# Mamba-2 layer of a diffusion trunk: z's in-projection tiles between the scan's steps, cumulated sums loaded by DMA, one exponential for both directions

## What is computed

```
proj = h @ w_in                       # z: 2048 columns, x: 2048, B: 1024, C: 1024, dt: 64
xbc  = silu(depthwise_conv(proj[x, B, C]))
dt   = softplus(dt_raw + dt_bias);  a = -exp(a_log)
# ssd_scan, for each direction, over chunks of 128 tokens, 8 groups of 4 heads:
acs    = cumsum(dt * a)                             # inside the chunk
decay  = exp(where(i >= j, acs_i - acs_j, -inf))
y_diag = ((C_i . B_j) * decay * dt_j) @ x
state  = state * exp(acs_last) + (exp(acs_last - acs) * dt * x)^T @ B
y_off  = (C_i . state) * exp(acs_i)
y      = rms_norm((y_f + flip(y_b) + x * skip) * silu(z), norm_g) @ w_out
```

## Time and profile before

| | us |
|---|---|
| median of 3 runs (2195.01 to 2195.77) | 2195.66 |
| the profiled execution: its own time | 2194.43 |
| its span, first to last instruction | 2192.7 |
| mean granted clock of PE over it | 0.959 |

### The profile page before, as it was taken

How to read it: one execution, slowest core, us unless ns; L and a number is a source line. 1 busy time by engine, 2 the same in 40 slices (tenths; PEclk the granted TensorE clock), 3 DMA queues, 4 the chain that set the end, 5 groups by cost and what they waited for, 6 DMA issues and landing times.

```text
span 2192.7 us, 30627 instructions
## 1 busy us (share of the span) xinstructions
PE 1998.8 (91%) x11880; PEld 1795.2 (82%) x11880; DVE 1295.2 (59%) x1942; ACT 976.0 (45%) x1703; POOL 745.2 (34%) x567
## 2 busy tenths in 40 slices
PE   3789999999978877999999995799999979899998
PEld 1579998799978866799987994599998766699986
DVE  0567761666338866677724797377751686577732
ACT  1344442544336633544424683354442535544432
POOL 0133324333326655333343730233334330333242
PEclk7889999999989989999999997999999988999999
DMA  9953346434310034544365500644446432244332
GB/s 371 383 208 124 124 132 233 165 124 125 125 58 30 31 121 173 221 144 125 116 230 175 203 11 0 278 173 125 125 164 221 147 111 82 81 145 125 125 125 77
DMA packets 77072, 320.96 MB, mean 146 GB/s; under 512 B 8672, under 2 KB 14208, under 8 KB 63104
## 3 DMA queue, kind: packets, MB, share of 16 engines
q1 hardware_dynamic: 76048, 318.18, 41.4%
q10 hardware_dynamic: 880, 0.82, 0.1%
HBM read 314.96 MB, written 4.01 MB: 145 GB/s over the span
## 4 chain that ended last, share of the span: by engine, by line
PE 72%; DVE 14%; ACT 5%; DMA 5%; issue 2%; POOL 1%; SPq 1%; DVEq 0%; ACTq 0%
PE pair L1675 15%; PE pair L1677 15%; PE pair L1676 15%; PE pair L1709 6%; PE pair L1711 6%; PE pair L1710 6%; DVE convolved L1484 5%; PE pair L1798 2%; DVE x L1246 2%; DMA mod_more<-in_w_mod 1%; PE pair L1831 1%; DMA raw<-in_pool 1%; DMA raw<-in_ssd_out 1%; ACT junk L848 1%; DVE w_lo L1179 1%
## 5 line engine op out<-in xcount | busy, mean ns | idle before, releaser
L675 POOL TENSOR_TENSOR w_lo<-raw,w_hi 128x512 fp32r<-128x512 f32 (+1 forms) x375 | 578.0, 1543 | 1205.9 <-ACT w_hi L820 1205.9
L1675 PE MATMUL pair<-h_hi,w_hi 128*128 128x386 f32 (+1 forms) x2008 | 686.6, 342 | 19.4 <-POOL h_lo L682 19.4
L1677 PE MATMUL pair<-h_hi,w_lo 128*128 128x386 f32 (+1 forms) x2008 | 682.6, 340 | 0.0
L1676 PE MATMUL pair<-h_lo,w_hi 128*128 128x386 f32 (+1 forms) x2008 | 681.9, 340 | 0.0
L1179 DVE TENSOR_TENSOR w_lo<-raw,w_hi 128x512 fp32r<-128x512 f32 x351 | 427.7, 1221 | 335.7 <-ACT w_hi L820 335.7
L820 ACT ACTIVATE w_hi<-raw 128x1024 fp32r<-128x1024 f32 x375 | 393.0, 1050 | 293.6 <-PE pair L1711 208.7
L1675 PEld LDWEIGHTS pair<-h_hi,w_hi 128*128 128x128 f32 (+1 forms) x2008 | 380.1, 189 | 24.2 <-POOL h_lo L682 22.9
L1676 PEld LDWEIGHTS pair<-h_lo,w_hi 128*128 128x128 f32 (+1 forms) x2008 | 380.7, 190 | 0.9
L1677 PEld LDWEIGHTS pair<-h_hi,w_lo 128*128 128x128 f32 (+1 forms) x2008 | 380.1, 189 | 0.3
L1303 DVE SCALAR_TENSOR_TENSOR acc<-pair,taps,acc 128x385 f32<-128x385 f32 x176 | 108.9, 619 | 212.6 <-ACT acc L907 212.6
L907 ACT ACTIVATE acc<-pair,taps 128x386 f32<-128x386 f32 x176 | 117.4, 667 | 236.1 <-PE pair L1677 236.1
(11 more groups left out here) (254 smaller groups left out, 2481.6 us busy)
## 6 DMA issues: line engine op xcount, KB each, us to landing
raw<-in_ffn_in SPq DMA_DIRECT2D x176, 512.0 KB, 3.5
raw<-in_ffn_out SPq DMA_DIRECT2D x88, 512.0 KB, 3.6
mod_raw<-in_w_mod SPq DMA_DIRECT2D x32, 1024.0 KB, 7.6
mod_base<-in_w_mod SPq DMA_DIRECT2D x31, 1024.0 KB, 7.5
mod_more<-in_w_mod SPq DMA_DIRECT2D x20, 1024.0 KB, 13.4
raw<-in_ssd_conv SPq DMA_DIRECT2D x32, 512.0 KB, 3.5
gb<-rows_dram SPq DMA_DIRECT2D x8, 1024.0 KB, 5.2
raw<-in_ssd_z SPq DMA_DIRECT2D x16, 512.0 KB, 3.5
```

Source lines behind the costliest of these rows:

```text
L675: pool.tensor_tensor(w_lo[:, m % SLOTS, 0:w], raw[:, m % SLOTS, 0:w], w_hi[:, m % SLOTS, 0:w].bitcast(F32), ALU.subtract).then_inc(w_low_p ...
L1675: ten.matmul(to, wh, h_hi[:, k, cols], start=k == 0, stop=False, skip_group_check=True)
L1676: ten.matmul(to, wh, h_lo[:, k, cols], start=False, stop=False, skip_group_check=True)
L1677: ins = ten.matmul(to, wl, h_hi[:, k, cols], start=False, stop=k == KD - 1, skip_group_check=True)
```

## The change

1. The tile of dt comes first, then 6 of the 16 tiles of z (Z_FIRST): one ahead of dt's turn, three beside DVE's softplus chain, two behind the cumulation. The other 10 tiles are cut into parts of three matmuls, 80 in all, and spread over the scan's steps 0 to 21, half of a step's parts ahead of its states and half behind. z_made(u) tells how many tiles are made after step u; a further one is complete after u = 2, 4, 6, 8, 10, 13, 15, 17, 19 and 21. ACT takes z out with a copy, and at these steps also rounds a weight chunk, and DVE, POOL and SP move their counters with it. SiLU of z is applied later, in ssd_end, one tile ahead.
2. The cumulated sums are made once, as rows (6 matmuls), for all heads and both directions. ACT copies them and exponentiates them (cum_rows), and stores both to DRAM (cum_dram, 2 x 96 KB). In each step SP loads the four heads' rows of both directions to all 128 partitions, 512 KB in pieces of 2 KB, into one of now four decay slots, and for latent chunks the exponentiated ones too, another 512 KB, into c_scaled. The 8 matmuls a step and ACT's exponentials of line 963 go away. A decay slot is loaded when the output of u - 4 has been made, a c_scaled slot when that of the same latent chunk one group earlier has.
3. ACT adds the partition's own sum (8 operations of 128 x 128, segments(), for the next step), DVE takes the smaller of the two directions (least(), 128 x 512), and ACT exponentiates that once. The masks pick the valid half for either direction.
4. Chunk 16 of the out-projection is loaded with the others, and round_to and low_to for it are moved into the loop over m.

The diff, cut to its core:

```
+SEG_SLOTS = 4
+Z_FIRST = 6
+Z_STEPS = 22
...
-            order += [Linear("ssd_conv", CONV_TILES), Linear("ssd_z", KI), Linear("ssd_dt", 1, KD * NDT),
+            order += [Linear("ssd_conv", CONV_TILES), Linear("ssd_dt", 1, KD * NDT), Linear("ssd_z", KI),
...
+        cum_dram = nc.dram_tensor("cum_dram", [2, 3, 2, GROUPS, HPG, P], F32, kind="Internal").ap()
...
-        decay = [by_dir(flat_mod[:, k * 1024:(k + 1) * 1024]) for k in range(SCAN_SLOTS)]
-        c_scaled = [by_dir(flat_mod[:, 3072:4096]), by_dir(flat_gb[:, 1024:2048])]
-        turned = flat_gb[:, 0:1024].rearrange("p (u n) -> p u n", u=2)
+        decay = [by_dir(flat_mod[:, k * 1024:(k + 1) * 1024]) for k in range(SEG_SLOTS)]
+        c_scaled = [by_dir(flat_gb[:, k * 1024:(k + 1) * 1024]) for k in range(2)]
+        turned = rowc[:, :].rearrange("p (u n) -> p u n", u=2)
+        cum_rows = flat_wk[0:NDT, 0:2 * 3 * P].rearrange("p (k c n) -> p k c n", k=2, c=3)
...
+        def z_made(u):
+
+            return divmod(Z_FIRST * KD + min((KI - Z_FIRST) * KD, (KI - Z_FIRST) * KD * (u + 1) // Z_STEPS), KD)
+
+        def z_bank(m):
+            return bank((2, 3, 7)[m % 3])
...
+                sp.wait_ge(cum_stored, 32)
+                for g, c, u, v in steps():
+                    if u >= SEG_SLOTS:
+                        sp.wait_ge(s_y, u - SEG_SLOTS + 1)
+                    sp.dma_start(decay[u % SEG_SLOTS], heads_rows(0, c, g)).then_inc(seg_loaded[u % SEG_SLOTS], 16)
+                    if c:
+                        if v >= 2:
+                            sp.wait_ge(s_y, latent_step(v - 2) + 1)
+                        sp.dma_start(c_scaled[v % 2], heads_rows(1, c, g)).then_inc(rise_loaded[v % 2], 16)
...
+                    load_to(z0 + z_made(u)[0] + SLOTS)
...
                     load_to(s.n0 + SLOTS)
-                    scan_traffic()
...
-                    load_to(s.n0 + 15)
+                    load_to(s.n0 + s.chunks)
                     sp.wait_ge(y_lo_ready, KI)
                     load_ends(2, 4, 5, 6)
-                    load_to(s.n0 + s.chunks)
                     sp.wait_ge(w_used, s.n0 + 11)
...
             def scan_pool():
...
                 for g, c, u, v in steps():
+                    low_to(z0 + z_made(u - 1)[0] + SLOTS)
...
                     if c:
+                        pool.wait_ge(rise_loaded[v % 2], 16 * (v // 2 + 1))
...
+            def z_evac(m):
...
+                act.wait_ge(w_used, s.n0 + m + 1)
+                act.activation(zt[:, m, :], z_bank(m)[:, 0:COLS], ACT.Copy).then_inc(evac, 1)
+                round_to(s.n0 + m + 5)
...
                 act.activation(rowc[:, 576:768], rowc[:, 384:576], ACT.Exp, scale=-1.0).then_inc(dt_act, 1)
+                for m in range(1, 4):
+                    z_evac(m)
+                act.wait_ge(dt_pe, 2)
+                rows = bank(4)[0:NDT, 0:3 * P].rearrange("p (c n) -> p c n", c=3)
+                act.activation(cum_rows[:, 0, :, :], rows, ACT.Copy).then_inc(cum_ready, 1)
+                act.activation(cum_rows[:, 1, :, :], rows, ACT.Exp).then_inc(cum_ready, 1)
+                for k in range(2):
+                    act.wait_ge(cum_ready, k + 1)
+                    act.dma_start(cum_dram[k, :, :, :, :, :].rearrange("c d g h n -> (d g h) c n"),
+                                  cum_rows[:, k, :, :]).then_inc(cum_stored, 16)
                 act.wait_ge(z_dt, DT_DVE - 1)
                 act.activation(to_end, to_end, ACT.Exp).then_inc(dt_act, 1)
                 act.activation(full_decay, full_decay, ACT.Exp).then_inc(dt_act, 1)
...
+                for m in range(4, Z_FIRST):
+                    z_evac(m)
...
+                def segments(g, c, u):
+                    act.wait_ge(seg_loaded[u % SEG_SLOTS], 16 * (u // SEG_SLOTS + 1))
+                    for d in range(2):
+                        for h in range(HPG):
+                            w = decay[u % SEG_SLOTS][:, d, h * P:(h + 1) * P]
+                            col = d * SSD_HEADS + g * HPG + h
+                            ins = act.activation(w, w, ACT.Identity, bias=neg_cum[:, c, col:col + 1])
+                    ins.then_inc(s_seg, 1)
+
+                segments(0, 0, 0)
...
                     act.activation(turned[:, u % 2, :], bank(u % 2), ACT.Copy).then_inc(s_copied, 1)
...
-                        w = decay[u % SCAN_SLOTS][:, d, :]
-                        act.activation(w, w, ACT.Exp, scale=-1.0 if d else 1.0).then_inc(s_exp, 1)
+                    act.wait_ge(s_least, u + 1)
+                    w = decay[u % SEG_SLOTS][:, 0, :]
+                    act.activation(w, w, ACT.Exp).then_inc(s_exp, 1)
+                    if u + 1 < len(ALL_STEPS):
+                        segments(*ALL_STEPS[u + 1][:3])
+                    while evacuated < z_made(u)[0]:
+                        z_evac(evacuated)
+                        evacuated += 1
...
+                act.activation(zt[:, 0, :], zt[:, 0, :], ACT.Silu).then_inc(z_silu, 1)
...
+                def least(u):
+                    vec.wait_ge(s_seg, u + 1)
+                    w = decay[u % SEG_SLOTS]
+                    vec.tensor_tensor(w[:, 0, :], w[:, 0, :], w[:, 1, :], ALU.min).then_inc(s_least, 1)
...
-                    for h in range(HPG):
-                        col = g * HPG + h
-                        ins = vec.tensor_scalar(decay[u % SCAN_SLOTS][:, 0, h * P:(h + 1) * P], bank(2)[:, h * P:(h + 1) * P],
-                                                neg_cum[:, c, col:col + 1], 0.0, ALU.add, ALU.min)
...
+                    ch.wait()
+                    vec.wait_ge(s_exp, u + 1)
+                    w = decay[u % SEG_SLOTS].rearrange("p d (h i) -> p d h i", h=HPG)
+                    for d in (1, 0):
+                        if d == 0:
+                            vec.wait_ge(s_w, 2 * u + 1)
+                        vec.tensor_tensor(w[:, d, :, :], w[:, 0, :, :], cb_mask[:, d, :].unsqueeze(1).broadcast_to(
+                            [P, HPG, P]), ALU.mult).then_inc(s_w, 1)
+                    if u + 1 < len(ALL_STEPS):
+                        least(u + 1)
                     if u >= SCAN_LAG:
                         output(*ALL_STEPS[u - SCAN_LAG][:3])
+                    low_to(z0 + z_made(u)[0] + SLOTS)
...
-                    if m + 3 < KI:
-                        low_to(n0 + m + 3)
+                    low_to(n0 + min(m + 3, KI))
...
+            def z_part(m, k):
+                z = lin["ssd_z"]
+                if k == 0:
+                    if m < 2:
+                        ten.wait_ge(conv_done, lin["ssd_conv"].conv0 + CONV_TILES - 3 + m)
+                    else:
+                        ten.wait_ge(evac, EVAC_Z + m - 2 if m > 2 else EVAC_DT + 1)
+                    chunk_ready(z.n0 + m)
+                ins = tile_part(z_bank(m)[:, 0:COLS], z.n0 + m, P, slice(0, COLS), k)
+                if k == KD - 1:
+                    ins.then_inc(w_used, 1)
+
+            def z_tiles(first, last):
+                for m in range(first, last):
+                    for k in range(KD):
+                        z_part(m, k)
...
             def dt_prepare():
+                dt = lin["ssd_dt"]
+                chunk_ready(dt.n0)
+                tile(bank(7)[0:NDT, 0:COLS], dt.n0, NDT, slice(0, COLS)).then_inc(w_used, 1)
+                z_tiles(0, 1)
...
                 ins.then_inc(dt_pe, 1)
+                z_tiles(1, 4)
...
                 for d in range(2):
                     hs = slice(d * SSD_HEADS, (d + 1) * SSD_HEADS)
+                    for c in range(3):
+                        ten.matmul(bank(4)[hs, c * P:(c + 1) * P], adt[:, c, hs], tri[:, d, :], start=True, stop=True,
+                                   skip_group_check=True)
...
                            start=True, stop=True, skip_group_check=True).then_inc(dt_pe, 1)
+                z_tiles(4, Z_FIRST)
...
+                    now, then = (KD * m + k for m, k in (z_made(u - 1), z_made(u)))
+                    for i in range(now, (now + then) // 2):
+                        z_part(*divmod(i, KD))
                     if u:
                         states((u - 1) % 3, u - 1)
-                    for d in range(2):
-                        if u:
-                            ten.wait_ge((s_seg, s_seg_back)[d], u)
-                        for h in range(HPG):
-                            col = d * SSD_HEADS + g * HPG + h
-                            ins = ten.matmul(bank(2 + d)[:, h * P:(h + 1) * P],
-                                             adt[:, c, col:col + 1].broadcast_to([P, P]), tri[:, d, :],
-                                             start=True, stop=True, skip_group_check=True)
-                        ins.then_inc(s_cum, 1)
+                    for i in range((now + then) // 2, then):
+                        z_part(*divmod(i, KD))
                     if u >= SCAN_LAG:
                         output(*ALL_STEPS[u - SCAN_LAG])
...
-                    ten.wait_ge(s_exp, 6 * GROUPS)
```

(1 more changed line is left out.)

145 lines of the change are left out of this document (52 added, 93 removed).

## The result

The changed kernel takes **2212.89 us** (median of 4 runs, 2210.88 to 2214.49) against 2195.72 us: a ratio of 1.0074, with a 95% interval of 1.0061 to 1.0086. It is 17 us slower. The forecast was 2161 us, 34 us faster. The profiled execution took 2213.61 us, 19.2 more than that of before.

The account below looks back on a forecast made before the run. PE was taken to bound the kernel (72% of the chain), with waits before and in the scan. Start -54.1, groups +25.7, tail -1.7, out-projection -4 sum to -34.1: 2161 us for the median, range 2132 to 2180.

Parts of the forecast that it names:

- The start: Scan's start: masks 50 us earlier, dt's wait covered by z tiles, third output at 621 in place of 675.1: -54.1 us.
- the fourth rival: z in the scan: not hidden, only moved, PE standing for chunks or banks; ends between the first two rivals; no chance given.
- The groups: Six groups of the scan: 123.0 us against 102.4, plus 5.1 for PE's slower clock: +25.7 us.
- 1.7 us for each further 512 KB: Row loads in each group: a second 512 KB behind the first adds 1.7 us to 3.5, so the decay slot lands after 5.2.
- the cycle: One group, output to output through load, ACT's additions, least and state: 18.3 us, PE standing 2.9 at its first latent output.
- The second rival: Scan: DVE becomes the bound, slowed by POOL; 23 us a group, +35.6 us, 2171 us; chance 0.20.
- the third rival: Scan: waits keep PE at half clock through whole groups, 28.9 us a group, 2207 us; chance 0.04.
- The clock: Scan groups: after waits of 3 to 6 us PE's granted clock falls in about half of the groups: +5.1 us.
- The tail: Scan's end, 21st output to the last: no z parts or sum matmuls left there, but the same clock fall: -1.7 us.
- The out-projection: Out-projection: chunk 16, loaded with the others, is there in time and PE's wait goes: -4 us.
- The first rival: Scan: loads in time and PE the bound, a group stays at 17.1 us, 2136 us; chance 0.22.

Follow-up runs that it names:

- e12: The changed kernel, with DVE making the low part of the chunk for the scan's first z tile ahead of its first least: 2207.51 us.
- e1: The changed kernel without loads of cumulated rows after four steps and of their exponentials after two latent steps (decays not the reference's): 2179.42 us.
- e4: The changed kernel, with DVE taking the next step's least behind the taking of the state: 2210.62 us.
- e10: e1 with POOL's product of c_scaled with C left out: 2143.47 us.
- e13: e1 with POOL filling c_scaled with a constant in place of multiplying it by C: 2144.58 us.
- e7: The kernel before, with only the out-projection's last chunk loaded with the others and rounded among the last gatings: 2188.97 us, ratio 0.9971.
- e11: e1 with all 16 tiles of z ahead of the scan: 2211.98 us.
- e15: The kernel before with dt first, chunk 16 loaded earlier, z's SiLU in the out-projection, sums still on PE, three z tiles in the scan's PE waits: 2166.37 us.

## Why the prediction was wrong

**The start, -54.1 forecast, -41.1 measured (-39.5 from the mixer's start).** The first half was exact: the first masks start at 597.2 us against 599.2, and counted from the mixer's start 50.4 us earlier than before, where 50 was forecast. Wrong was what follows, "its third output ends 21.8 us after the first masks": it took 36.8, because "PE starts warm and has z's parts to fill with" did not hold. PE's next part of z waited 8.67 us for a low part that stands in DVE's program behind masks, products and least; the fourth rival saw "no such wait". Then the first latent output waited 6.20 us for POOL. e12 takes the first wait away and gets back 7.0 us of the 14.6 at this place; behind it the first latent output still waits 6.5 us, for DVE, and is slow.

**The groups, +25.7 forecast, +56.2 measured.** The failed step is the load: "1.7 us for each further 512 KB". I took the lower end of the price of 2 KB pieces by analogy with 8 KB pieces, and the upper end, 0.7 us more, was too low as well: a load moves in 3.2 us or more. In the six groups the decay rows land 7.4 to 10.9 us after their issue, where the cycle has 5.2. By e1 the loads cost 28 us of the groups. The path itself, from the output through the rows, ACT's additions, least and the taking of the state to the next output, is the one in the trace. That the place of least in DVE's program makes it, as the cycle says, is not: e4 moved it and won 2 us, since the products behind it need the same load.

A second step failed with it: the sum has one cycle, the one through the load, and puts PE ready for the output at 7.0 us where nothing else is waited for. POOL's row isn't in it. Without the loads the groups take 130.8 us, close to my 123.0 + 5.1 with loads, and that is luck: it is POOL's row that holds them, not the cycle. Loads at the forecast price would have left that row as the bound.

**The second rival** (DVE bound by POOL, chance 0.20, 23 us a group) saw the meeting of the two engines: in e1 leasts take 1.22 us and products 1.18. It put the bound at DVE, and e1's waits put it at POOL, whose products went from 1.2 to 1.54 us. Treated as a rival instead of a term to be added, it left the sum without it. Slower had a chance of 0.04 in all, for the third rival alone, because each cost stood in a case of its own; they happened at once.

**The clock, +5.1 forecast for half of the groups.** It fell in all of them: the first latent outputs take 3.80 to 4.69 us where 2.54 is full speed, 10.8 us more in the six groups (12.7 with the one before them). The third rival (half speed through whole groups) did not come, though its 2207 us is the nearest to the time measured: the granted clock is 0.82 over the groups, and the second output of each group takes 2.57 us, as before. The other end of the same term: in the six groups of e10 and e13 waits of up to 1.9 us leave the clock at 1.00, and this whole cost is gone.

**The tail, -1.7 forecast, +4.7 measured**: the last group goes through the same waits and slow output (4.39 us, then 6.03 for the last 64 matmuls, which took 6.81 before), and PE waits 8.02 us more for DVE's taking of a state at 802.95.

**The out-projection, -4 forecast**: -6.3 in the profile, -4.4 in e7's profile and -6.4 in e7 by its ratio. The mechanism was right, and the size is inside what these three allow.

**The first rival** (17.1 us a group, 2136): z's parts do hide, as e11 and e15 show; PE was never the bound of the changed scan.

## What to carry to other kernels

Work taken off the bounding engine must be paid for where it lands: here 5.4 us of matmuls a group became a transfer that every step waits for, additions on ACT and one more pass over SBUF on DVE, and the transfer and the pass became longer by meeting other work. POOL, which got only the low parts of z, became the bound of what was left, by its own work and by DVE's. When two costs can both happen, add them; a rival that needs nothing but the change itself is a term. Follow the row of every engine round the cycle, not only that of the transfer. To tell whether an engine's work or something else binds, look at who releases the waits, before and behind the edit: a shorter operation that gains nothing more may only have met the next bound. Try the parts apart: the reordering that cost nothing (dt first, the chunk earlier, three tiles of z in PE's own waits) was worth 29 us (e15); the change, which has the first two, the moved sums and ten tiles of z in the scan, is 46 us behind that.
